# One inference step of a two-layer mLSTM and pooling decoder on one core: a rebuilt beginning, and accumulators read one by one

## The chip, the core and the metric

The kernel runs on one core of a Trainium2 chip. Its engines are TensorE (PE, with the weight loads listed apart as PEld), VectorE (DVE), ScalarE (ACT), GpSimd (POOL) and SyncE (SP, which only issues DMAs here); each runs its own list of instructions in order, and semaphores tie the lists together. The metric is the device time of one execution in microseconds (us): the median of three runs of the kernel before is 2596.98 us (2596.16 to 2598.49).

## The reference, cut to what matters

One step of a decoder with two layers, on a prompt (16 meta tokens and 256 prompt tokens) and on a sample group (8 sequences of 8 tokens): 336 columns in all, each of width D = 2048. Layer 0 mixes tokens by an mLSTM (4 heads, keys of 256, values of 512, with a matrix state C per sequence), layer 1 by pooling; behind each stands a gated feed-forward network (FFN) of width 5504 with a short convolution.

```python
def trunk(x, ...):
    for layer in range(DEPTH):
        u = rms_norm(x, norm_mix[layer])
        if layer % 2 == 0:
            y, (C, n, m) = mlstm_mixer(u, w_mlstm_in, b_mlstm_gate, g_mlstm_out, w_mlstm_out, (C, n, m), lead)
        else:
            y, pbuf = pool_mixer(u, st_pool, pos0, w_pool, pool_scale)
        x = x + y
        u = rms_norm(x, norm_ffn[layer])
        y, cbuf = conv_ffn(u, st_conv, w_up, conv_w, conv_b, w_down)
        x = x + y
    out = rms_norm(x, norm_final)

def mlstm_mixer(u, w_in, ...):
    q, k, v, o, gates = split(u @ w_in)          # gates: 4 input and 4 forget gates per column
    ig, lf = gates[:H] + b, log_sigmoid(gates[H:] + b)
    # running sums of lf, running maxima m_t (the stabilisers), scores exp(d - m_t), state C, n
```

For the beginning this matters: u is x over its root mean square per column times a gain per feature, and the gates, with all the row tables of running sums and maxima made from them, need u @ w_in for eight columns of w_in. All of it is float32.

## The kernel before, in words

**Products.** x is held with features on partitions (16 blocks of 128 features, 336 columns). The product of a weight block with x is made in three passes of TensorE over split numbers: a weight w is split into a high half wh and the rest wl, x into xh and xl, and wh·xh, wh·xl and wl·xh are summed (lines 433 to 435). The gain of the norm is multiplied into xh and xl, while the factor per column (one over the root mean square, `rbc`) is applied when an accumulator is read.

**Chunks.** Weights come in chunks of 256 rows by 512 columns (0.5 MB), by SyncE's `chunk` (line 287), into four slots. ScalarE writes the high half of a chunk (`hi`, line 814), VectorE the low half (`lo`, line 1081), and each counts a semaphore: `raw_landed`, `hi_done`, `lo_done`, and `chunk_used` once TensorE is done with it. `gemm` works through the chunks of a product; each chunk is 24 passes, six for each of four accumulators, SA[0..3] or SB[0..3] (the eight banks); products alternate between SA and SB.

```python
                for i in range((nkt + 1) // 2):
                    if amid and i in amid:
                        amid[i]()
                    s = (k0 + i) % SLOTS
                    pe.wait_ge(lo_done, c + (k0 + i + 1))
                    if fresh:
                        fresh(2 * i)
                    for t in range(nt):
```

`amid[i]` is other work of TensorE put ahead of chunk i, `guard` and `free` are waits of an accumulator's first pass, and `fresh` waits for the split x. A head of the mLSTM is a product of eight chunks for q and k (SA, chunks 0 to 7), one of eight for v (SB, chunks 8 to 15), one for the output gate (SA, 16 to 23), and four of two chunks each for the output projection. VectorE reads accumulators in order and counts `evac`; before the change it begins on the four of a product when `chunk_used` says that the last chunk is done, as in `add_to_x` (line 1100), which adds the output projection or an FFN's down projection to x.

**The beginning.** SyncE issues five DMAs for x with tokens on rows, in whole rows (lines 299 to 303), twelve for the parameters of norms, convolutions and the normaliser state n (`in_par`, lines 304 to 314), those of the gates (`in_gate`, 315 to 321), then chunks. TensorE transposes x (line 472) as the three row blocks arrive, then the parameters (477 to 484); it makes the gates, eight columns of w_in spread over 36, in full float32 (490), and sums squares over the features by 16 products with a matrix of ones (494). Only then comes the first `gemm`. ScalarE writes four chunk halves and then, by turns, the high half of a block of x and its square (857 to 865); VectorE copies the transposed x out of the banks (1103 to 1107), scales the gate weights (1120), and writes chunk halves and the low half of x. The row tables (1127 to 1143, tables of 4 rows by 336) wait once for ScalarE's exp and ln (868, 871). Head 0's TensorE list then turns the row tables into columns (`stabilisers`, ahead of chunk 5).

**Later places that the change touches.** Line 513, in `new_states`: the products of the new state C of the previous head, which stand between the chunks of a head's q and k product. Line 628: the products of the prompt's state, between the output gate product and the output projection; they wait for accumulators SA[2] and SA[3]. Lines 1334 and 1337: VectorE's read of an FFN's second product (`fh`) and the low half made of it (`hl`), which the down projection takes. Line 799: the final transposes; line 782: the last sums of squares of the second norm, with a sum made on GpSimd (line 1486).

## Time and profile before

| | |
|---|---|
| median of three runs | 2596.98 us |
| the profiled execution | 2595.99 us |
| its span (first to last instruction in the trace) | 2593.6 us |
| TensorE busy | 98% of the span |
| VectorE, ScalarE, GpSimd busy | 53%, 38%, 7% |
| first pass over a weight chunk starts at | 46.07 us |

All times in a trace count from the start of the span. The profiled execution lasted 2.4 us longer than its span: what lies ahead of its first and behind its last instruction. A row of a timeline gives the start and the duration of an instruction, or of a run of like ones, its engine and line, its tiles (written<-read) and, in brackets, how long the engine stood idle ahead of it and what ended that. Passes of TensorE are pipelined: one is listed with 0.3 to 0.6 us, but the next starts before it ends; so a cost per pass is taken from a stretch over a count and not from the duration of one.

### The profile page before, as it was taken

To read this page: it belongs to the slowest core of one execution; us is meant where nothing else is said; L and a number is where in the kernel's file an instruction comes from. 1 tells how busy PE (TensorE), PEld (TensorE's weight loads), DVE (VectorE), ACT (ScalarE), POOL (GpSimd) and SP (SyncE) were. 2 spreads that over 40 slices of the span, in tenths; PEclk is the share of its full clock that TensorE was granted. 3 is DMA by queue.
4 is the path that set the end of the run, shared out by engine and by line. 5 is a ranking of instruction groups with operands and counts; after the bars stand their busy time and mean duration, and the time that the engine had idled before them with its cause. 6 is when DMAs were issued, how large, how long until landed. Compare 5 with 4: busy or idle time off the path is not lost. (4 is left out here: it accounts for less than half of the span.)

```text
span 2593.6 us, 43931 instructions
## 1 busy us (share of the span) xinstructions
PE 2554.5 (98%) x16751; PEld 2481.2 (96%) x16751; DVE 1364.6 (53%) x2095; ACT 976.1 (38%) x1284; POOL 172.8 (7%) x338
## 2 busy tenths in 40 slices
PE   7999999999999999999999999999999999999998
PEld 5989898998999999999999999999999999999998
DVE  5445464547654454544544546755554554545545
ACT  4332323235432333433333335543333333433435
POOL 1000000002060000000000002300000000000002
PEclk9999999999999999999999999999999999999999
DMA  4637364563544444444444444344444444444443
GB/s 129 203 113 253 102 225 137 158 216 109 202 142 144 142 144 140 137 151 147 142 145 142 144 127 149 117 147 149 155 148 154 149 149 150 143 161 151 148 136 109
DMA packets 226617, 389.63 MB, mean 150 GB/s; under 512 B 25564, under 2 KB 55636, under 8 KB 225876
## 3 DMA queue, kind: packets, MB, share of 16 engines
q1 hardware_dynamic: 214683, 367.26, 44.5%
q10 hardware_dynamic: 11736, 19.67, 2.1%
q8 instruction: 132, 2.16, 0.3%
q14 instruction: 66, 0.54, 0.1%
HBM read 363.86 MB, written 23.43 MB: 149 GB/s over the span
## 5 line engine op out<-in xcount | busy, mean ns | idle before, releaser
L1081 DVE TENSOR_TENSOR w_lo<-w_raw,w_hi 128x1024 fp32r<-128x1024 f32 x664 | 814.8, 1233 | 971.4 <-ACT w_hi L814 968.9
L814 ACT ACTIVATE w_hi<-w_raw 128x1024 fp32r<-128x1024 f32 x664 | 700.0, 1059 | 1356.2 <-PE bank L435 1325.7
L433 PE MATMUL bank<-xh,w_hi 128*128 128x336 f32 (+2 forms) x3584 | 1131.9, 316 | 0.7 <-DVE w_lo L1081 0.5
L434 PE MATMUL bank<-xl,w_hi 128*128 128x336 f32 (+2 forms) x3584 | 1125.3, 314 | 0.0
L435 PE MATMUL bank<-xh,w_lo 128*128 128x336 f32 (+2 forms) x3584 | 1123.5, 313 | 0.0
L433 PEld LDWEIGHTS bank<-xh,w_hi 128*128 128x128 f32 x3584 | 673.1, 188 | 17.5 <-issue 15.4
L434 PEld LDWEIGHTS bank<-xl,w_hi 128*128 128x128 f32 x3584 | 674.2, 188 | 1.2 <-issue 1.0
L435 PEld LDWEIGHTS bank<-xh,w_lo 128*128 128x128 f32 x3584 | 674.9, 188 | 0.0
L433 PE MATMUL bank<-hh,w_hi 128*128 128x336 f32 (+1 forms) x1632 | 513.0, 314 | 4.5 <-issue 4.5
L435 PE MATMUL bank<-hh,w_lo 128*128 128x336 f32 (+1 forms) x1632 | 511.4, 313 | 0.0
L434 PE MATMUL bank<-hl,w_hi 128*128 128x336 f32 (+1 forms) x1632 | 511.2, 313 | 0.0
L433 PEld LDWEIGHTS bank<-hh,w_hi 128*128 128x128 f32 x1632 | 306.9, 188 | 6.0 <-issue 6.0
L434 PEld LDWEIGHTS bank<-hl,w_hi 128*128 128x128 f32 x1632 | 307.4, 188 | 1.0 <-issue 1.0
L435 PEld LDWEIGHTS bank<-hh,w_lo 128*128 128x128 f32 x1632 | 307.9, 189 | 0.0
L1526 POOL COPY area<-area 128x18 f32<-128x18 f32 x86 | 37.1, 434 | 1703.2 <-DVE area L1313 1703.2
L1100 DVE TENSOR_TENSOR x<-bank,x 128x336 f32<-128x336 f32 (+1 forms) x256 | 110.4, 494 | 69.3 <-PE bank L435 69.3
L974 ACT ACTIVATE area<-area 128x352 f32<-128x352 f32 (+1 forms) x86 | 42.4, 493 | 58.3 <-DVE area L1321 58.3
L980 ACT ACTIVATE hh<-area 128x336 fp32r<-128x336 f32 (+1 forms) x86 | 36.5, 478 | 67.1 <-DVE area L1334 67.1
L1481 POOL TENSOR_TENSOR area<-area 128x336 f32<-128x336 f32 x58 | 57.7, 995 | 33.9 <-ACT area L842 26.9
L1288 DVE SCALAR_TENSOR_TENSOR area<-area,bank 128x512 f32<-128x512 f32 x64 | 43.6, 744 | 20.0 <-PE bank L513 19.9
L969 ACT ACTIVATE area<-area,cp 128x352 f32<-128x352 f32 (+1 forms) x86 | 50.9, 663 | 5.8 <-DVE area L1313 5.8
L1334 DVE TENSOR_TENSOR area<-bank,area 128x336 f32<-128x336 f32 (+1 forms) x86 | 37.0, 492 | 27.7 <-PE bank L435 27.7
(268 smaller groups left out, 1021.0 us busy)
## 6 DMA issues: line engine op xcount, KB each, us to landing
w_raw<-in_w_up SPq DMA_DIRECT2D x640, 256.0 KB, 2.8
w_raw<-in_w_down SPq DMA_DIRECT2D x336, 256.0 KB, 3.4
w_raw<-in_w_mlstm_in SPq DMA_DIRECT2D x192, 256.0 KB, 3.4
area<-in_state_mlstm_C SPq DMA_DIRECT2D x32, 512.0 KB, 7.4
w_raw<-in_w_mlstm_out SPq DMA_DIRECT2D x64, 256.0 KB, 3.2
out_C_sample<-area ACTq DMA_DIRECT2D x32, 512.0 KB, 5.8
w_raw<-in_w_up SPq DMA_DIRECT2D x64, 192.0 KB, 2.5
w_raw<-in_w_pool SPq DMA_DIRECT2D x16, 256.0 KB, 3.0
```

What stands on the lines that cost most here:

```text
L433: pe.matmul(out, wh, xhk, start=first, stop=False)
L434: pe.matmul(out, wh, xlk, start=False, stop=False)
L435: return pe.matmul(out, wl, xhk, start=False, stop=last)
L814: nc.scalar.activation(w_hi[:, s], w_raw[:, s], ACT.Copy).then_inc(hi_done, 1)
L969: nc.scalar.activation(Tt[:, t, a0:GW - 2], E[:, t, a0 + 2:GW], ACT.Identity, bias=cp[:, 3, 4 * q + t:4 * q + t + 1], scale=cp[:, 2, 4 * q ...
L974: nc.scalar.activation(Tt[:, t, a0:GW - 2], Tt[:, t, a0:GW - 2], ACT.Silu).then_inc(silu_ready, 1)
L1081: V.tensor_tensor(w_lo[:, s], w_raw[:, s], w_hi[:, s].bitcast(F32), ALU.subtract).then_inc(lo_done, 1)
L1100: V.tensor_tensor(x[:, 4 * n + t, c0:], banks[t][:, c0:T], x[:, 4 * n + t, c0:], ALU.add).then_inc(evac, 1)
L1288: V.scalar_tensor_tensor(Cr[b][:, k], Cr[b][:, k], WI[:, NS * b + NS - 1:NS * b + NS], SB[s][:, :], ALU.mult, ALU.add).then_inc(c_updated, 1)
L1334: V.tensor_tensor(fh[:, t, a0:], SB[t][:, a0:T], Sp[:, t, a0:], ALU.mult).then_inc(evac, 1)
L1481: m_ = G.tensor_tensor(sums[k], sums[k], squares[k][:, kt % 4], ALU.add)
L1526: m_ = G.tensor_copy(last[:, q, 0:nt * ROWS].rearrange("p (b s f) -> p b s f", s=2, f=nt)[:, :, :, t], E[:, t, NP - NS:].rearrange("p (b s ...
```

## The change

**The beginning.** SyncE brings x in three pieces of columns (features 0 to 511, 512 to 1023, 1024 to 2047), with two q and k chunks of head 0 between them; the gates' weights, the convolution tables and n stand behind chunks 5 and 6, and the norms' parameters are issued by ScalarE. TensorE turns the identity 22 times, the norms' parameters and the first quarter of x, and goes into head 0's q and k product; the other three quarters of x stand ahead of its chunks 1, 2 and 3, the gates ahead of chunk 5, the row scales ahead of chunk 6 and the remaining parameters ahead of chunk 7. The gates are now summed in four strips of 32 columns (each strip over four of the 16 blocks), copied out by ScalarE and added by one more product with a table `pick`. The sum of squares of a column is made by ScalarE on x with tokens on rows (`row_squares`, the sum beside the square), its root and inverse on three columns, and TensorE spreads the inverse over all partitions by a product with a diagonal (`row_scales`). The column tables (`columns`) move behind the end of the q and k product, ahead of the v product's chunk 1, and the scores from chunk 2 of the v product to chunk 4.

**Reads one by one.** TensorE counts `acc_done` after the last pass of each accumulator of a product but the last one, and VectorE waits for that count ahead of each read (`summed`) and no longer for the end of the whole product. This is done for all products of the heads, the FFNs and the pooling layer. The first product of line 628 now waits for the third read of four, and the order of reads at the output gate becomes 0, 1, 2, 3.

```diff
+            def x_piece(p):
+                cols = PIECES[p]
+                for rows, s, src in ((slice(0, META), 0, I["meta_tokens"]), (slice(META, P), 0, I["x_prompt"][0, 0:P - META]),
+                                     (slice(0, P), 1, I["x_prompt"][0, P - META:2 * P - META]),
+                                     (slice(0, META), 2, I["x_prompt"][0, 2 * P - META:SEQ]),
+                                     (slice(META, TL), 2, I["x_sample"].rearrange("b s d -> (b s) d"))):
+                    sp.dma_start(xtok[rows, s, cols], src[:, cols]).then_inc(in_x[p], 16)
...
+            x_piece(0)
+            qk_chunk(0, 0, 0)
+            qk_chunk(0, 0, 1)
+            x_piece(1)
+            qk_chunk(0, 0, 2)
+            qk_chunk(0, 0, 3)
+            x_piece(2)
+            qk_chunk(0, 0, 4)
+            qk_chunk(0, 0, 5)
...
+            qk_chunk(0, 0, 6)
+            for i in range(2):
...
+                        if i == (nkt + 1) // 2 - 1 and t < nt - 1:
+                            mm_.then_inc(acc_done, 1)
...
+            def to_features(q):
+                pe.wait_ge(in_x[min(q, 2)], 16 * 5)
+                for s, (t0, m) in enumerate(TOK):
+                    n = 3 * q + s
+                    if n == 3:
+                        pe.wait_ge(st_ev, 1)
+                    elif n > 3:
+                        turned(n - 4)
                     for t in range(4):
                         kt = 4 * q + t
-                        m_ = pe.transpose(bank[(4 * s + q) % 8][:, t * P:t * P + n], xtok[0:n, s, kt * P:(kt + 1) * P],
-                                          ident[0:n, 0:n])
+                        m_ = pe.transpose(SB[n % 4][:, t * P:t * P + m], xtok[0:m, s, kt * P:(kt + 1) * P], ident[0:m, 0:m])
                     m_.then_inc(st_tr, 1)
...
+            def gates():
+                turned(9)
+                turned(10)
+                turned(11)
+                pe.wait_ge(wgg_ready, 1)
+                for k in range(KT // 4):
+                    for s in range(4):
+                        kt = 4 * k + s
+                        m_ = pe.matmul(SB[3][32 * s:32 * s + 32, 0:T], wgg[:, kt, :], x[:, kt, :], start=(k == 0),
+                                       stop=(k == KT // 4 - 1), skip_group_check=True)
+                m_.then_inc(gates_mm, 1)
+            def row_scales():
+                pe.wait_ge(rdiag_ready, 1)
+                for s, (t0, n) in enumerate(TOK):
+                    m_ = pe.matmul(SB[0][:, t0:t0 + n], ones[0:n, :], rdiag[0:n, s, 0:n], start=True, stop=True)
+                m_.then_inc(rbc_mm, 1)
...
+            def parameters():
...
+            for _ in range(WARM):
+                pe.transpose(SA[0][:, 0:P], ident[:, :], ident[:, :])
+            pe.wait_ge(in_par, 16 * 5)
+            pe.transpose(SB[3][:, 0:7 * KT], ptok, ident[0:7 * KT, 0:7 * KT]).then_inc(st_tr, 1)
+            to_features(0)
...
+                def columns():
+                    pe.wait_ge(rows_ready, 1)
+                    pe.wait_ge(evac, e + 4)
...
+                if first:
+                    gemm(SA, c, 0, KT, 4, xh, xl, 0, fresh=lambda kt: pe.wait_ge(xl_done, kt + 2),
+                         amid={1: lambda: to_features(1), 2: lambda: to_features(2), 3: lambda: to_features(3), 5: gates,
+                               6: row_scales, 7: parameters})
+                    guard = {0: (r_ready, 1), 1: (rows_ready, 1), 2: (st_ev, 10), 3: (st_ev, 11)}
...
-                gemm(SB, c, 8, KT, 4, xh, xl, 0, free=None if first else after(e - 4), guard=guard, amid={2: scores})
+                gemm(SB, c, 8, KT, 4, xh, xl, 0, free=None if first else after(e - 4), guard=guard,
+                     amid={1: columns, 4: scores} if first else {2: scores})
...
-                    pe.wait_ge(evac, e + (8 + (1, 4)[k]))
+                    pe.wait_ge(evac, e + (8 + (3, 4)[k]))
...
+                for s, (t0, n) in enumerate(TOK):
+                    if p + s:
+                        act.wait_ge(row_sq, 3 * p + s)
+                    nc.scalar.activation(spent[0:n, 0:cols.stop - cols.start], xtok[0:n, s, cols], ACT.Square,
+                                         accum_out=parts[0:n, s, p:p + 1]).then_inc(row_sq, 1)
...
+            hi(0, 0)
+            gather(0)
+            x_high(0)
+            hi(0, 1)
+            hi(0, 2)
+            gather(1)
+            x_high(1)
+            act.wait_ge(consts, 2)
+            row_squares(0)
+            hi(0, 3)
+            gather(2)
+            x_high(2)
+            row_squares(1)
+            hi(0, 4)
+            gather(3)
+            x_high(3)
+            hi(0, 5)
+            row_squares(2)
+            hi(0, 6)
+            act.wait_ge(row_sum, 1)
+            nc.scalar.activation(rtok[:, 1], rtok[:, 0], ACT.Sqrt, bias=eps[:, :], scale=1.0 / D).then_inc(rt_ready, 1)
+            hi(0, 7)
...
+            def summed(t, nt, a, c):
+                if t < nt - 1:
+                    dve.wait_ge(acc_done, a + (t + 1))
+                else:
+                    dve.wait_ge(chunk_used, c)
...
+            def add_to_x(banks, n, c0, a, c):
                 for t in range(4):
+                    summed(t, 4, a, c)
...
+            lo(0, 5)
+            dve.wait_ge(row_sq, 9)
+            step(V.tensor_tensor(rtok[:, 2], parts[:, :, 0], parts[:, :, 1], ALU.add))
+            V.tensor_tensor(rtok[:, 0], rtok[:, 2], parts[:, :, 2], ALU.add).then_inc(row_sum, 1)
             dve.wait_ge(in_gate, 16 * 5)
             dve.wait_ge(consts, 2)
...
+            V.tensor_tensor(wgg[:, :, 0:8], wgr, par[:, 0:KT].unsqueeze(2).to_broadcast([P, KT, 8]), ALU.mult).then_inc(wgg_ready, 1)
+            lo(0, 6)
...
+                los(c, 9, 11)
                 if first:
                     dve.wait_ge(cleared, 1)
...
-                dve.wait_ge(chunk_used, c + 8)
                 for t in range(4):
+                    summed(t, 4, a, c + 8)
...
+                if first:
+                    dve.wait_ge(gcol_mm, 1)
+                    V.tensor_copy(gcol[:, :].rearrange("p s a h -> p (s a h)"), SA[1][:, 0:24]).then_inc(gcol_a, 1)
+                    lo(c, 12)
+                    dve.wait_ge(gcol_em, 1)
+                    scales(h, SA[3])
...
-                    dve.wait_ge(chunk_used, c + (k0 + nd))
-                    add_to_x((SA, SB)[n % 2], n, a0)
+                    add_to_x((SA, SB)[n % 2], n, a0, a + (ab + 3 * n), c + (k0 + nd))
```

TensorE's list from its start to the first weight passes, before (each row an operation, its tiles, its shape and how often it stands there in a row):

```order
L428 UNCONDITIONAL_BRANCH
L472 MATMUL bank<-ident,area 128x128 x32
L472 MATMUL bank<-ident,area 128x80 x16
L477 MATMUL bank<-ident,area 128x112
L480 MATMUL bank<-ident,area 128x86 x4
L484 MATMUL bank<-ident,area 128x32 x2
L490 MATMUL bank<-x,area 36x336 x16
L494 MATMUL bank<-area,ones 128x336 x16
L433 MATMUL bank<-xh,w_hi 128x336
```

The same stretch after the change:

```order
L458 UNCONDITIONAL_BRANCH
L553 MATMUL bank<-ident 128x128 x22
L555 MATMUL bank<-ident,area 128x112
L514 MATMUL bank<-ident,area 128x128 x8
L514 MATMUL bank<-ident,area 128x80 x4
L463 MATMUL bank<-xh,w_hi 128x336
```

48 transposes of x, the gates and 16 products for the sums of squares stood ahead of the first weight pass (L433 before, L463 after); now 12 transposes of x do, and the rest has moved between the chunks or, with the sums of squares, off TensorE.

ScalarE's list from its start, before (L814 is a chunk's high half, L860 the high half of a block of x, L863 a block's square):

```order
L804 UNCONDITIONAL_BRANCH
L814 ACT_TABLE_LOAD
L814 ACTIVATE w_hi<-w_raw 128x1024 x4
L860 ACTIVATE xh<-x,par 128x336
L863 ACTIVATE area<-x 128x336
```

After the change, from the chunk halves 1 and 2 to chunk half 3 (L884 is a chunk's high half, L932 the copy of transposed sample columns, L941 the high halves, L950 the squares of x by rows):

```order
L884 ACTIVATE w_hi<-w_raw 128x1024 x2
L932 ACTIVATE x<-bank 128x4x80
L941 ACTIVATE xh<-x,par 128x336 x4
L950 ACTIVATE area,parts<-area 128x512 x2
L950 ACTIVATE area,parts<-area 80x512
L884 ACTIVATE w_hi<-w_raw 128x1024
```

Where four chunk halves stood at the head of the list, chunk halves, the copies and high halves of a quarter of x, and the squares of a piece now alternate; the squares of the last piece stand behind six chunk halves (the diff has the whole order).

VectorE's list between the row tables and the reads of head 0's q and k product, before (L1149 is the last step ahead of the stabilisers, L1081 a chunk's low half, L1153 the copy of the column tables, L1166 to L1170 the scalings made from them, L1178 the first read of a q accumulator):

```order
L1149 TENSOR_SCALAR mrows<-mrows,negeye 4x336
L1081 TENSOR_TENSOR w_lo<-w_raw,w_hi 128x1024 x5
L1153 COPY gcol<-bank 128x24
L1157 COPY hcol<-gcol 128x6
L1158 COPY mbh<-mb 128x8
L1159 COPY nh<-nT 128x16
L1160 COPY gh<-par 128x4
L1166 TENSOR_SCALAR area<-bank,hcol 128x272
L1167 TENSOR_SCALAR area<-bank,hcol 128x144
L1168 TENSOR_SCALAR area<-bank,hcol 128x16
L1169 TENSOR_SCALAR area<-bank,hcol 128x4x16
L1170 TENSOR_TENSOR area<-bank,mbh 128x64
```

After the change (L1295 and L1297 copy the convolution tables and n, L1303 is the step ahead of the stabilisers, L1202 a chunk's low half, L1315 and L1316 the first of the reads):

```order
L1295 COPY cpar<-bank 128x344
L1297 COPY nT<-bank 128x64
L1303 TENSOR_SCALAR mrows<-mrows,negeye 4x336
L1202 TENSOR_TENSOR w_lo<-w_raw,w_hi 128x1024 x2
L1315 SCALAR_TENSOR_TENSOR area<-bank,rbc 128x272
L1316 SCALAR_TENSOR_TENSOR area<-bank,rbc 128x4x16
```

Five chunk halves and the scalings stood between the row tables and the reads; now two chunk halves do, and the copy of the column tables with the scalings has moved behind the reads (the last but one piece of the diff).

## Rows read from the trace of the kernel before

**Rows 1.** Page of before: busy us, share of span and instructions of each engine.
```profile
PE 2554.5 (98%) x16751; PEld 2481.2 (96%) x16751; DVE 1364.6 (53%) x2095; ACT 976.1 (38%) x1284; POOL 172.8 (7%) x338
```

**Rows 2.** Busy time by stretches: start:end, length, each engine (instructions), clock, DMA share, GB/s.
```profile
23.84:46.00 22.16, 22.09 (x63) 9.37 (x64) 13.78 (x20) 18.14 (x37) 0.96 (x1) 0.91 0.53 167
46.00:77.20 31.20, 31.20 (x204) 30.39 (x203) 18.70 (x35) 14.46 (x17) 0.00 (x0) 1.00 0.38 114
77.20:109.30 32.10, 32.10 (x212) 31.94 (x212) 13.76 (x24) 9.36 (x10) 2.23 (x4) 1.00 0.77 253
1581.00:1584.40 3.40, 3.40 (x14) 3.40 (x13) 1.03 (x1) 0.00 (x0) 0.00 (x0) 0.50 0.24 77
```

**Rows 3.** Timeline of TensorE, beginning: sample rows of x turned; first weight product.
```profile
13.01 1.33 PE L472 MATMUL bank<-ident,area 80*128 80x80 f32 x16 [0.26 <-DMA area<-in_x_sample]
...
46.07 0.57 PE L433 MATMUL bank<-xh,w_hi 128*128 128x336 f32 x1
```

**Rows 4.** Groups of TensorE instructions, 0 to 110 us: busy, mean, idle before.
```profile
L490 PE MATMUL bank<-x,area 128*36 128x336 f32 x32 | 11.2, 519 | 2.9 <-DVE area L1120 2.9
...
L472 PE MATMUL bank<-ident,area 128*128 128x128 f32 x32 | 5.4, 350 | 7.3 <-POOL area L1468 7.3
...
L477 PE MATMUL bank<-ident,area 112*128 112x112 f32 x1 | 0.4, 448 | 5.2 <-DMA area<-in_state_mlstm_n 5.2
```

**Rows 5.** Waits of TensorE over the span: us in total, times, longest.
```profile
PE bank L513 <- DVE x L1100: 3.0, 4, 1.8
...
PE bank L628 <- DVE area L1258: 2.8, 4, 0.7
```

**Rows 6.** Timeline of TensorE, down projection of FFN 0: start, us, line, [idle].
```profile
1580.24 0.39 PE L433 MATMUL bank<-hh,w_hi 128*128 128x336 f32 x1 [2.31 <-issue]
...
1581.39 0.48 PE L433 MATMUL bank<-hh,w_hi 128*128 128x336 f32 x1
...
1581.67 0.48 PE L434 MATMUL bank<-hl,w_hi 128*128 128x336 f32 x1
```

**Rows 7.** Timeline of TensorE at the end of the kernel.
```profile
2577.70 1.42 PE L799 MATMUL bank<-ident,x 128*128 128x128 f32 x11 [0.36 <-DVE x L1100]
...
2580.78 0.98 PE L782 MATMUL bank<-ones,area 128*128 128x1 f32 x6 [1.66 <-POOLq L1486]
```

**Rows 8.** DMA, 0 to 40 us: GB/s in 40 slices of one microsecond.
```profile
GB/s 0 41 188 295 319 279 287 410 442 164 221 143 54 17 40 25 45 59 53 4 1 46 214 325 324 303 378 370 238 357 168 335 254 286 285 300 45 0 0 0
```

**Rows 9.** Groups of ScalarE instructions by shape, 0 to 130 us.
```profile
L814 ACT ACTIVATE w_hi<-w_raw 128x1024 fp32r<-128x1024 f32 x23 | 24.2, 1057 | 61.7 <-PE bank L435 37.4 <-DMA w_raw<-in_w_mlstm_in 24.3
...
L860 ACT ACTIVATE xh<-x,par 128x336 fp32r<-128x336 f32 x16 | 8.9, 559 | 0.0
...
L910 ACT ACTIVATE area<-bank 128x512 f32<-128x512 f32 x2 | 1.2, 597 | 2.6 <-PE bank L584 1.5 <-PE bank L586 1.1
```

**Rows 10.** Groups of VectorE instructions by shape, 0 to 110 us.
```profile
L1081 DVE TENSOR_TENSOR w_lo<-w_raw,w_hi 128x1024 fp32r<-128x1024 f32 x19 | 23.1, 1224 | 26.7 <-ACT w_hi L814 26.5
...
L1090 DVE SCALAR_TENSOR_TENSOR xl<-x,par,xh 128x336 fp32r<-128x336 f32 x16 | 9.0, 568 | 5.1 <-ACT xh L860 5.1
...
L1106 DVE COPY x<-bank 128x512 f32<-128x512 f32 x8 | 5.2, 686 | 8.9 <-PE bank L472 8.9
```

**Rows 11.** Groups of TensorE instructions by shape: products into strips of 32 columns.
```profile
L598 PE MATMUL bank<-area 128*32 128x512 f32 x128 | 14.6, 595 | 0.0
```

**Rows 12.** Timeline of VectorE: first, middle and last row of the row tables.
```profile
51.12 0.50 DVE L1130 SCALAR_TENSOR_TENSOR area<-area 4x336 f32<-4x336 f32 x1
...
54.06 0.50 DVE L1132 SCALAR_TENSOR_TENSOR area<-area 4x336 f32<-4x336 f32 x1 [2.44 <-ACT area L869]
...
58.30 0.18 DVE L1142 COPY area<-mtrow 4x64 f32<-4x64 f32 x1
```

**Rows 13.** Timeline of VectorE ahead of the down projection after FFN 0.
```profile
1577.97 1.34 DVE L1334 TENSOR_TENSOR area<-bank,area 128x336 f32<-128x336 f32 x3 [0.41 <-PE bank L435]
...
1579.22 1.33 DVE L1337 TENSOR_TENSOR hl<-area,hh 128x336 fp32r<-128x336 f32 x3
```

352 lines of the change are left out of this document (190 added, 162 removed).

## The prediction

> **What bounds the kernel now.** I read the busy shares first: TensorE is busy 98% of the span, no other engine over 53% [rows 1]. So only time in which TensorE does something else than weight products, or waits, can be won. The windows by stage come next. In 46 to 77.2 us (head 0's q and k product) and 77.2 to 109.3 us (its v product) TensorE has no idle time at all [rows 2]; each window holds eight chunks of 24 products. The first product of a weight starts only at 46.07 us, though [rows 3]: 46 of 2593.6 us pass in getting ready. Of these, 22.2 us (23.84 to 46) are TensorE working, but on the gates and on the column sums of squares [rows 2], 32 passes of 11.2 us for the gates alone [rows 4]; and 5.2 us are a wait for the last of the parameter DMAs [rows 4]. That is the stage that the first part of the change rebuilds. The second part touches the ends of the products, and there the list of waits says what can be had: TensorE waits 2.8 us at line 628 and 3.0 us at line 513 for VectorE's reads of accumulators, in four places each [rows 5], some 2.3 us ahead of the last down projection of an FFN [rows 6], and little at the end [rows 7].
>
> **The first part, as a new timetable up to the end of head 0's v product (before: 109.3 us).** I lay the new order of each engine over durations of these rows.
>
> *Until the first weight product.* The DMAs move, in KB by microsecond, 41, 188, 295, 319, ... [rows 8]: 0.52 MB by 4 us, 1.12 MB by 6, 1.41 MB by 7. Columns 0 to 511 of x are 0.69 MB, chunk 0 behind them 0.52 MB: moved by 4.6 and 6.3 us. Before, all 2.75 MB of x are moved at about 11.9 us and TensorE is released at 13.0 [rows 3, 8], so a landing is seen about 1.1 us later: 5.7 and 7.4 us. TensorE meanwhile turns the identity 22 times and the parameters once (32 passes took 5.4 us, 0.17 each [rows 4]: 3.9 us), then the first quarter of x: 12 transposes, 2.0 us, done at about 8.4. ScalarE splits chunk 0 (1.06, to 8.5), copies the sample columns (about 0.5, to 9.0) and writes two high halves of x (0.56 each [rows 9], to 10.1). VectorE copies two groups (0.69 each), writes the low half of chunk 0 (1.22) and two low halves of x (0.57 each [rows 10]) to about 11.0. First weight product: 11 us instead of 46.
>
> *What TensorE then has to do up to the end of the v product.* The two windows of before, 31.2 + 32.1 = 63.3 us [rows 2], hold all that is still there (the small transposes of the row tables and the stabilisers' broadcast move from the first to the second). New between the chunks are: three quarters of x to turn, 36 transposes, 36 x 0.14 = 5.0 us (between 0.17 and the 0.11 that transposes take later on); the gates in four strips; the row scales (4 small products, 1.2 us); the last parameters (6 transposes, 1.0 us). The gates are 16 products of two passes. Passes of 32 columns in strips took 14.6 us for 128 of 512 columns [rows 11], 0.114 each, by 336/512 that is 32 x 0.075 = 2.4 us; if the strips do not run side by side, it is the 11.2 us of before [rows 4]. I take 2.4. Sum: 63.3 + 9.6 = 72.9; without a wait the v product ends at 84.
>
> *Waits that come in.* (a) The gates now stand ahead of chunk 5 and need the gate weights times the norm's gain, which VectorE writes only after ScalarE's ninth row square. ScalarE's list up to there: 6 chunk halves (1.06), 4 copies (0.5), 16 high halves (0.56), 6 squares of 512 columns (0.60 and reading the sum [rows 9], 0.7) and 3 of 1024 (1.2), 25 us less some 2.5 for overlap. It starts at 7.4 and is stopped about 9 us more, because it waits in its own order for transposes of quarters that TensorE issues only between chunks, and twice for VectorE's copies, queued behind a chunk's low half: 39 us, the gate weights at 39.6. TensorE is there at 11 + 5 x 3.7 + 5.0 = 34.5. Wait 5.0 (0 if ScalarE isn't stopped, 10 if twice as long). (b) Accumulator 1 of the v product waits for the finished row tables. Before, that chain took from 51.1 to 58.5 us, 2.44 of it waiting for ScalarE's exp and ln [rows 12]; now a chunk half stands in that gap on each engine. From the row scales (46.9 us) I come to 56.6, TensorE is there at 56.1: wait 0.6. (c) The column tables are turned ahead of chunk 9 and need all four q and k accumulators read. VectorE does the row tables to 56.6, two copies and a scaling (1.0), two chunk halves (2.4) and only then the four reads (2.0): 62.0. TensorE is there at 59.4: wait 2.6. Behind it, nothing but chunk 9 and the products after it. Together with 0.4 for a late chunk: 8.6 us.
>
> *The clock.* In 23.84 to 46 us the granted clock averages 0.91, in the two product windows it is 1.00; after the idle 2.3 us ahead of 1580.24 [rows 6] it is 0.50 for 1581 to 1584.4 [rows 2], half speed, 1.2 GHz. There 14 products took 3.40 us and not the 0.153 each of 46 to 77.2: 1.3 us lost. The new beginning has gaps of 2.4 us (8.4 to 11), 5.0 and 2.6: two or three such stretches, 3 us (0 to 9).
>
> End of the v product: 11 + 72.9 + 8.6 + 3 = 95.5, against 109.3: **13.8 us won** (19 without the clock's part and wait (b, c); 6 with the clock low through five chunks more).
>
> *What is hidden.* The 32-byte gate weights and the tables now stand between chunks 5, 6 and 7 on SyncE's queue. Before, that group ran at 4 to 59 GB/s for 9 us (12 to 21 us [rows 8]). From 14 us that makes chunk 7 land at about 28; ScalarE reaches it at 41. Only with 13 us more would it cost.
>
> **The second part: reads one by one.** The first three accumulators of a product end 2.8, 1.8 and 0.9 us before the fourth, and a read takes 0.45 [rows 13]; so behind the last product one read is left where there were four (or three). Line 628: its first product needs the third read, its second set the fourth: the 2.8 us [rows 5] go. Line 513: of 3.0 us I take 2.0; in one place low halves of x stand on VectorE ahead of it. Last down projections: three reads (1.34 us) and then the low halves [rows 13] become one read: 1.1 us twice, 2.2, and the stretch at 0.50 after the first of them in one case of two, 0.7. End: the last square and with it the sum on GpSimd come 1.2 us earlier of the 0.36 and 1.66 waited [rows 7]. Sum 8.9 us. From below it is 0 (if what TensorE waits for next is just as late), from above 12. VectorE now sits in an open wait between reads; behind it stand chunk halves, which had been behind the same reads before, so none gets later.
>
> **Sum.** 13.8 + 8.9 = 22.7. The profiled execution took 2595.99 us (span 2593.6), the median of the runs is 1.0 above it: 2596.98 - 22.7, about 2574 us.
>
> A rule that speaks against the new beginning: the Trainium skill, "TensorE: Matmul & The Clock Gate", section "HAM oscillation — how this bites in real kernels", tells of a kernel whose bursts of products are parted by waits of a few microseconds and in which every burst starts at the low clock. The trace agrees in one place, 0.50 after 2.3 us of idleness [rows 2, 6]. The sum above carries it as 3 us; the second rival below is what it would do at its worst.
>
> **Rivals.**
> 1. Only the beginning pays; the reads one by one uncover the next wait. For it: TensorE's whole list of waits is short [rows 5]. Against it: after the reads come 12 products of line 628 that cover ScalarE's and VectorE's next work. Then 2597 - 13.8, about 2583.
> 2. Slower: in the new beginning TensorE never works long enough in one piece, and its clock stays at half through both products of head 0. At half clock products start 0.28 apart (1581.39, 1581.67 [rows 6]), so a chunk takes 24 x 0.127 = 3.05 us longer, 16 chunks 49, less the 8.6 of waits that it covers: the v product ends at 133, 24 later than before, and with 8.9 won the time is about 2612. It turns at ten or eleven cold chunks. Against it: the gaps lie between pieces of 18 us and more without a pause, and a slower TensorE leaves fewer gaps.
> 3. The gaps on ScalarE are longer (the squares, the strips not side by side, chunks late): some 8 us more before the gates or in them: about 2582.
> 4. Neither the clock nor waits (b) and (c) show: about 2567.
>
> **How the numbers follow.** The forecast has 0.70 with 2566 to 2581 as its own range; rival 1 has 0.09, rival 3 0.10, rival 4 0.07, rival 2 0.03, and 0.01 is left for no change. 2564 to 2586 holds the forecast, 1, 3 and 4 but for their tails, some 0.85. A difference under 0.2%, 5 us, can't be told from none: faster 0.95, same 0.02, slower 0.03.
>
> **What would show it.** The first weight product at 10 to 13 us; a wait of 3 to 7 us ahead of the gates; a wait of 1 to 4 ahead of the column tables; the end of the v product at 91 to 100; granted clock 0.5 in two or three stretches before 60 us and 1.0 from then on. Line 628 without a wait for VectorE; the idle time ahead of the last down projections at 1.2 and not 2.3. Wrong it is if the v product ends after 103, or if TensorE's waits after 110 us are no shorter than before.

## The result

The changed kernel takes 2578.31 us (median of four runs, 2577.53 to 2579.03) against 2596.57 us (2595.63 to 2598.49) of the kernel before on the same chip: 18.3 us or 0.7% less, a ratio of 0.9932 (95% interval 0.992 to 0.9944). Forecast were 2574 us and a range of 2564 to 2586; the gain was put at 22.7 us. The profiled execution took 2579.03 us, its span went from 2593.6 to 2577.0 us.

The page of the changed kernel, busy time and share of the span by engine; its counterpart is [rows 1]:

```profile
PE 2544.0 (99%) x16749; PEld 2480.5 (96%) x16749; DVE 1363.0 (53%) x2095; ACT 981.4 (38%) x1291; POOL 154.3 (6%) x332
```

TensorE is busy for 10.5 us less, of the 16.6 that the span lost; the rest was idle time. Where it came from is seen best by the same piece of work at the same point of both lists; the differences add up down the table:

| TensorE starts | before, us | after, us | ahead by |
|---|---|---|---|
| the first weight pass | 46.07 | 11.86 | 34.2 |
| head 0's `values` (the transposes of v), in its output gate product | 112.79 | 102.85 | 9.9 |
| head 0's prompt state | 154.19 | 143.40 | 10.8 |
| the last head's prompt state | 598.54 | 585.01 | 13.5 |
| the work behind FFN 0's down projection | 1602.12 | 1586.16 | 16.0 |
| the convolution tails in FFN 1's last pass | 2541.19 | 2524.91 | 16.3 |
| the transposes at the end | 2575.76 | 2560.70 | 15.1 |
| the end of the span | 2593.6 | 2577.0 | 16.6 |

The beginning gave 9.9 us, the places of the prompt state 0.9 us each, FFN 0's tail about 2; FFN 1's tail cost 1.2, and the end gave 1.5. Of FFN 0's tail about 1.3 us (14 passes in 3.40 us, at 0.153 each without the low clock [rows 2]) are half clock that stands there in the kernel before and not here; FFN 1's tail is the reverse. The last section shows that this differs between kernels with the same code at that place, so these two rows hold some chance. Rows of TensorE's timeline after the change (start, duration, instruction, in brackets the idle time ahead and what ended it), beginning:

```profile
11.86 0.39 PE L463 MATMUL bank<-xh,w_hi 128*128 128x336 f32 x1 [3.33 <-DVE xl L1211]
33.03 0.42 PE L463 MATMUL bank<-xh,w_hi 128*128 128x336 f32 x1 [0.99 <-DVE w_lo L1202]
41.32 4.71 PE L526 MATMUL bank<-x,area 128*32 128x336 f32 x32 [4.37 <-DVE area L1262]
...
61.31 0.42 PE L463 MATMUL bank<-xh,w_hi 128*128 128x336 f32 x1 [0.55 <-DVE area L1292]
66.68 0.19 PE L589 MATMUL bank<-ident,area 4*128 4x4 f32 x1 [2.33 <-DVE area L1320]
```

The first weight pass, where [rows 3] had 46.07, starts at 11.86; then come a late chunk, the wait for the gate weights (L1262 is their scaling), the row tables (L1292) and the reads of the q and k accumulators (L1320). The granted clock of the new beginning, in windows (start:end, length, busy time and count of TensorE, weight loads, VectorE, ScalarE, GpSimd, then clock, DMA share, GB/s), which answers to [rows 2]:

```profile
12.40:15.80 3.40, 3.40 (x14) 3.40 (x14) 2.18 (x3) 1.49 (x2) 0.00 (x0) 0.50 1.10 326
39.70:46.50 6.80, 5.18 (x34) 2.12 (x35) 3.88 (x9) 4.72 (x8) 0.00 (x0) 0.50 0.57 156
67.00:73.80 6.80, 6.80 (x25) 5.89 (x24) 4.63 (x16) 1.97 (x4) 0.00 (x0) 0.50 0.74 241
80.00:95.00 15.00, 15.00 (x102) 14.84 (x101) 5.87 (x7) 4.89 (x6) 3.79 (x4) 1.00 0.84 275
```

Three stretches at 1.2 GHz, each in or behind one of the gaps of 3.3, 4.4 and 2.3 us, 17 us in all. Two short ones, 3.4 us each, follow later, from 627 and from 2538 us, and the last 4.6 us of the span are at half clock too. The waits of TensorE (total, times, longest), to be laid beside [rows 5]:

```profile
PE bank L526 <- DVE area L1262: 4.4, 1, 4.4
PE bank L463 <- issue: 3.7, 2, 1.9
...
PE bank L574 <- DVE x L1229: 3.0, 4, 1.8
PE bank L589 <- DVE area L1320: 2.3, 1, 2.3
```

The wait of line 628 (L698 now) is gone; that of line 513 (L574 now) stands as before, 3.0 us.

### The profile page after: what moved, and what is told of

It reads as the page before. It is cut to its first block and busy times, and to the rows that moved or that the text cites. A ratio compares the mean times of both kernels' runs of the same rounds, so it can differ in the third digit from the quotient of the medians.

```text
span 2577.0 us, 44182 instructions
## 1 busy us (share of the span) xinstructions
PE 2544.0 (99%) x16749; PEld 2480.5 (96%) x16749; DVE 1363.0 (53%) x2095; ACT 981.4 (38%) x1291; POOL 154.3 (6%) x332
## 5 line engine op out<-in xcount | busy, mean ns | idle before, releaser
L1202 DVE TENSOR_TENSOR w_lo<-w_raw,w_hi 128x1024 fp32r<-128x1024 f32 x664 | 812.3, 1228 | 1064.7 <-ACT w_hi L884 1064.1
L884 ACT ACTIVATE w_hi<-w_raw 128x1024 fp32r<-128x1024 f32 x664 | 699.8, 1058 | 1360.8 <-PE bank L465 1350.2
L463 PE MATMUL bank<-xh,w_hi 128*128 128x336 f32 (+2 forms) x3584 | 1135.9, 317 | 5.4 <-DVE xl L1211 3.3
L463 PEld LDWEIGHTS bank<-xh,w_hi 128*128 128x128 f32 x3584 | 675.6, 189 | 24.7 <-issue 17.7
L463 PE MATMUL bank<-hh,w_hi 128*128 128x336 f32 (+1 forms) x1632 | 513.2, 314 | 3.7 <-issue 3.7
L463 PEld LDWEIGHTS bank<-hh,w_hi 128*128 128x128 f32 x1632 | 307.0, 188 | 5.2 <-issue 5.1
L1688 POOL COPY area<-area 128x18 f32<-128x18 f32 x86 | 22.7, 266 | 1717.1 <-DVE area L1469 1717.1
L1477 DVE SCALAR_TENSOR_TENSOR area<-area,cp 128x352 f32<-128x352 f32 (+1 forms) x86 | 49.6, 577 | 3.1
```

The lines of the kernel that those rows point to most:

```text
L463: pe.matmul(out, wh, xhk, start=first, stop=False)
L884: nc.scalar.activation(w_hi[:, s], w_raw[:, s], ACT.Copy).then_inc(hi_done, 1)
L1202: V.tensor_tensor(w_lo[:, s], w_raw[:, s], w_hi[:, s].bitcast(F32), ALU.subtract).then_inc(lo_done, 1)
L1477: V.scalar_tensor_tensor(Tt[:, t, a0:GW - 2], E[:, t, a0:GW - 2], cp[:, 0, f:f + 1], Tt[:, t, a0:GW - 2], ALU.mult, ALU.add).then_inc(taps ...
```

## The experiments

Each of these eight kernels is the changed kernel with the edit shown; lines that only follow from the ones shown are left out (in run one ScalarE's order and waits, in run seven which partitions are copied and added). The first four ran on one chip, the last four on another. The times of the kernel before that ran beside them are 2596.01 us (first four) and 2595.69 us (last four), so differences between the groups of runs are good to about 1 us. Executions of one kernel lie up to 5 us apart.

**One: the reads undone.** Theory: the change's two parts add up, and about half of what the reads give comes from the prompt state.

```diff
             def summed(t, nt, a, c):
-                if t < nt - 1:
-                    dve.wait_ge(acc_done, a + (t + 1))
-                else:
-                    dve.wait_ge(chunk_used, c)
+                dve.wait_ge(chunk_used, c)
...
-                    pe.wait_ge(evac, e + (8 + (3, 4)[k]))
+                    pe.wait_ge(evac, e + (8 + (1, 4)[k]))
...
-                for f in range(4):
+                for f in (2, 0, 1, 3):
                     summed(f, 4, a + 6, c + 24)
```

> The changed kernel with only its second part undone: VectorE again waits for the whole product ahead of the first read, and the read order at the output gate and the wait of the prompt's state products are those of before. Theory A (sizes read from the two traces: about 9.9 us come from the beginning, 3.6 from the four places of the prompt's state products, the rest of 16.6 from the tails and the end): about 2584.5 us, 6 to 7 above the changed kernel's 2578.3, the state products waiting 0.7 us each again. Theory B (the sizes of the forecast, 8.9 us for the reads): 2587. Theory C (the reads one by one bring nothing, all comes from the beginning): 2578.

Measured: 2585.72 us (2583.92 to 2588.17), ratio to before 0.9958 (0.9945 to 0.9972). So the beginning alone is worth 10.3 us (against the kernel before beside it) and the reads 7.4 (against the changed kernel) or 8.0 (what 10.3 leaves of 18.3). The list of waits has the prompt state's again:

```profile
PE bank L698 <- DVE area L1398: 2.8, 4, 0.7
```

The row has the number of [rows 5], in four places as there. The time lies between theory A (2584.5) and theory B (2587) and does not tell them apart; theory C and the forecast's first rival (only the beginning pays) are out.

**Two: the gate weights early.** One multiplication of VectorE is moved ahead of its wait for ScalarE's ninth row square, and also ahead of the low halves of x's last quarter and of chunk 5.

```diff
             gather(3)
+            dve.wait_ge(in_gate, 16 * 5)
+            dve.wait_ge(consts, 2)
+            dve.wait_ge(st_ev, 1)
+            V.tensor_tensor(wgg[:, :, 0:8], wgr, par[:, 0:KT].unsqueeze(2).to_broadcast([P, KT, 8]), ALU.mult).then_inc(wgg_ready, 1)
             x_low(0, 0, 0, 12, 16)
...
             V.tensor_tensor(rtok[:, 0], rtok[:, 2], parts[:, :, 2], ALU.add).then_inc(row_sum, 1)
-            dve.wait_ge(in_gate, 16 * 5)
-            dve.wait_ge(consts, 2)
-            dve.wait_ge(st_ev, 1)
-            V.tensor_tensor(wgg[:, :, 0:8], wgr, par[:, 0:KT].unsqueeze(2).to_broadcast([P, KT, 8]), ALU.mult).then_inc(wgg_ready, 1)
             lo(0, 6)
```

> The changed kernel with one instruction moved: VectorE scales the gate weights right after the copies of the last quarter of x, ahead of the low halves of that quarter and of chunk 5, no longer behind the nine row squares. Theory A (the wait ahead of the gates is VectorE's order alone, and the low clock in the gates follows from that wait): TensorE goes into the gates at about 37 us and not at 41.3, the 32 passes take about 2.3 us and not 4.7, some 1 us of wait appears ahead of the row scales; together 5 to 6 us, about 2573. Theory B (the strips take 0.56 us a round at any clock): 4.4 less 1, about 2575. Theory C (the row sums, not the gate weights, set the pace, and the wait only moves to the row scales): within 1 us of 2578.

Measured: 2569.13 us (2568.56 to 2573.47), 9.2 less than the changed kernel, ratio to before 0.9902 (0.9887 to 0.9917). TensorE's timeline, gates, row scales and column tables, and two windows:

```profile
37.94 2.47 PE L526 MATMUL bank<-x,area 128*32 128x336 f32 x32
45.09 0.90 PE L534 MATMUL bank<-area,ones 128*128 128x128 f32 x6 [0.77 <-DVE area L1267]
61.85 0.19 PE L589 MATMUL bank<-ident,area 4*128 4x4 f32 x1 [2.33 <-DVE area L1320]
```

```profile
59.60:61.80 2.20, 0.00 (x0) 0.00 (x0) 2.20 (x10) 0.00 (x0) 0.00 (x0) 1.00 0.85 221
61.85:69.00 7.15, 7.15 (x48) 6.69 (x49) 4.98 (x16) 2.92 (x5) 0.00 (x0) 1.00 0.72 236
```

The gates start without a wait and take 2.47 us, half of 4.71: that is the clock. The row scales wait 0.77 us, as expected. More came than theory A's 5 to 6 us, for the second window: TensorE stands still for 2.33 us ahead of the column tables as it did in the changed kernel, but here the clock stays at 1.00 behind it, some 3 us that were not counted on and that the edit was not meant to bring. Head 0's `values` start at 94.93 us, 7.9 earlier, and the lead is still 8.0 at the convolution tails of FFN 1's last pass (2516.94 us); the rest lies behind them, where the changed kernel has a stretch at half clock from 2538 us and this one none, though both wait 1.88 us there.

**Three: the gaps filled.** No wait is shortened; transposes that nobody reads keep TensorE at work.

```diff
             to_features(0)
+            for _ in range(28):
+                pe.transpose(SA[0][:, 0:P], ident[:, :], ident[:, :])
...
                 turned(11)
+                for _ in range(38):
+                    pe.transpose(SB[3][:, 0:P], ident[:, :], ident[:, :])
                 pe.wait_ge(wgg_ready, 1)
...
+                    pe.wait_ge(evac, e + 1)
+                    for _ in range(12):
+                        pe.transpose(SA[0][:, 0:P], ident[:, :], ident[:, :])
                     pe.wait_ge(evac, e + 4)
```

> The changed kernel with TensorE kept busy in its three gaps by transposes of the identity that nobody reads: 28 behind the first quarter of x, 38 ahead of the wait for the gate weights, 12 ahead of the column tables. No wait is shorter. Theory A (the three stretches at a granted clock of 0.50, from 12.4, 39.7 and 67.0 us, come from TensorE standing idle, and cost 1.5, 2.3 and 3 us): the clock stays at 1.00, the gates take 2.3 us, and the time falls by 5 to 7 us, to about 2572. Theory B (the clock falls for something else, for example at a set time after the start): the stretches at 0.50 stay and the time is within 1 us of 2578, or longer by what the transposes overrun.

Measured: 2573.95 us (2570.72 to 2575.97), 4.4 less than the changed kernel, ratio 0.9916 (0.9903 to 0.993). From the timeline and the windows of TensorE:

```profile
11.95 0.39 PE L463 MATMUL bank<-xh,w_hi 128*128 128x336 f32 x1 [0.19 <-DVE xl L1218]
22.74 1.37 PE L514 MATMUL bank<-ident,area 128*128 128x128 f32 x12 [1.92 <-DMA area<-in_x_sample]
37.80 4.31 PE L523 MATMUL bank<-ident 128*128 128x128 f32 x38
42.04 2.47 PE L528 MATMUL bank<-x,area 128*32 128x336 f32 x32
```

```profile
11.90:15.90 4.00, 3.95 (x26) 3.97 (x27) 2.19 (x3) 2.10 (x3) 0.00 (x0) 1.00 1.12 307
24.20:27.60 3.40, 3.40 (x14) 3.40 (x13) 2.75 (x6) 2.75 (x6) 0.00 (x0) 0.50 0.26 33
66.00:72.00 6.00, 6.00 (x40) 6.00 (x41) 3.83 (x15) 2.92 (x5) 0.00 (x0) 1.00 0.93 294
```

The gates start 0.7 us later than in the changed kernel and take 2.47 us: their 4.71 was the clock and nothing else. All three stretches at 0.50 are gone, and a new one stands behind a new gap: chunk 0, at full speed, brings TensorE to the third quarter of x before its last DMA has landed (1.92 us), and there the clock falls. Why 4.4 and not 5 to 7 us came is seen on VectorE, where the gate weights are scaled (the changed kernel's row first, then this run's):

```profile
40.88 0.29 DVE L1262 TENSOR_TENSOR area<-area,par 128x128 f32<-128x128 f32 x1
...
39.44 0.29 DVE L1269 TENSOR_TENSOR area<-area,par 128x128 f32<-128x128 f32 x1
```

They are ready 1.4 us earlier: after a chunk 0 at full speed the second quarter of x is turned at 15.73 us and not at 17.16, and ScalarE and VectorE keep that lead. TensorE, though, is at its 38 transposes until 42.04 us, 2.3 us after the weights are there (39.73). So the low clock in chunk 0 does cost 1.4 us, and the transposes that overrun give 2.3 away; without them some 6.7 us would have come, an estimate from these rows. The Trainium skill, "TensorE: Matmul & The Clock Gate", section "Part 4: PE-mode transpose", says that the full clock does not engage for transposes. This run does not agree: with 38 of them in 4.31 us the granted clock is 1.00 up to and through the gates, in the window below (whether they run in the mode that the page means, the trace does not tell).

```profile
37.80:44.45 6.65, 6.65 (x73) 5.03 (x70) 3.88 (x9) 4.75 (x8) 0.00 (x0) 1.00 0.61 173
```

**Four: chunk halves behind the reads.** What came of the reads in the output projection and in the FFNs' tails?

```diff
                 for n in range(4):
-                    los(c, 28 + 2 * n, 30 + 2 * n)
+                    lo(c, 28 + 2 * n)
                     add_to_x((SA, SB)[n % 2], n, 0, a + (9 + 3 * n), c + (26 + 2 * n))
+                    lo(c, 29 + 2 * n)
...
-                    los(c, k0 + 12, k0 + 19)
+                    tail = nt < 4
+                    los(c, k0 + 12, k0 + (18 if tail else 19))
...
+                    if tail:
+                        for f, t in ((product, 0), (product, 1), (low, 0), (low, 1), (product, 2), (low, 2)):
+                            f(t)
+                        lo(c, k0 + 18)
```

Here `product` is the read of an accumulator and `low` the low half made from it, both as they were.

> The changed kernel with VectorE's list changed at two places: in the output projection the low half of the later of two chunks stands behind the four reads and not ahead of them, and in the last pass of each FFN the low half of one chunk stands behind the reads, with the first two low halves of the activations ahead of the third read. Theory A (there the reads one by one could not begin early, because a chunk half stands ahead of them that waits for the end of the product itself): the 3.0 us of waits ahead of the new state's products, in four places, fall to about 0.5, the two idle times of 1.8 and 1.9 us ahead of the last down projections to about 0.8, and with the stretches at half clock that follow them the time falls by 4 to 6 us, to about 2573. Theory B (the next wait is just as late, a chunk's low half now): within 1 us of 2578.

Why it was expected is seen in the changed kernel's own trace: VectorE's timeline around the end of head 0's output projection (TensorE leaves its last product at 178.3 us), and ScalarE's:

```profile
179.50 1.23 DVE L1202 TENSOR_TENSOR w_lo<-w_raw,w_hi 128x1024 fp32r<-128x1024 f32 x1 [2.50 <-ACT w_hi L884]
180.64 1.74 DVE L1229 TENSOR_TENSOR x<-bank,x 128x336 f32<-128x336 f32 x4
```

```profile
178.41 1.06 ACT L884 ACTIVATE w_hi<-w_raw 128x1024 fp32r<-128x1024 f32 x1 [2.66 <-PE bank L465]
```

The low half needs ScalarE's high half, which needs the slot of the product's last chunk. It cannot run before the product ends, and the four reads stand behind it. Measured: 2572.44 us (2572.01 to 2575.14), 5.9 less than the changed kernel, ratio 0.9915 (0.9901 to 0.9928). VectorE at the same place, and the waits of TensorE at line 574 and ahead of the last down projections:

```profile
175.74 1.93 DVE L1229 TENSOR_TENSOR x<-bank,x 128x336 f32<-128x336 f32 x4
178.32 1.23 DVE L1202 TENSOR_TENSOR w_lo<-w_raw,w_hi 128x1024 fp32r<-128x1024 f32 x1 [0.65 <-ACT w_hi L884]
```

```profile
PE bank L574 <- DVE area L1445: 2.0, 1, 2.0
PE bank L463 <- issue: 1.6, 2, 0.8
```

The reads now run beside the product. The wait for them at line 574 is gone (one of 2.0 us for VectorE's state update is left), and 3.7 us ahead of the down projections became 1.6. Theory A; of the 5.9 us some 1.2 may be chance, since head 0's `values`, ahead of the first place that the edit touches, already start at 101.67 us and not at 102.85: the gates had half clock for 3.4 us only.

**Five: the three orders together**, the two above and the column tables ahead of chunk 10:

```diff
-                     amid={1: columns, 4: scores} if first else {2: scores})
+                     amid={2: columns, 4: scores} if first else {2: scores})
```

> The changed kernel with three orders changed together: the gate weights scaled early (the run before: 9.2 us), the chunk halves behind the reads in the output projection and in the last pass of each FFN (5.9 us), and the column tables turned ahead of chunk 10 and not of chunk 9, so that chunk 9 covers the reads that they wait for (2.3 us of idle time). Theory A (the three are independent waits of TensorE, so their gains add up): 2578.3 - 9.2 - 5.9 - 2.3, about 2561 us. Theory B (what is taken out of one place comes back as a wait for chunk halves or for the row tables in the next): above 2566.

Measured: 2561.23 us (2560.68 to 2562.26), 17.1 less than the changed kernel and faster than both kernels; ratio to before 0.9867 (0.9852 to 0.9882). The gains add up as expected, with the wait of 2.3 us alone counted for the third order; what that order gives by itself is in run eight. The windows from the gates to the first part of the output gate product:

```profile
37.60:40.10 2.50, 2.50 (x34) 1.04 (x34) 1.23 (x1) 2.44 (x6) 0.00 (x0) 1.00 0.07 20
60.00:66.00 6.00, 6.00 (x42) 5.32 (x41) 3.87 (x10) 1.16 (x2) 0.00 (x0) 1.00 0.48 140
66.00:92.00 26.00, 26.00 (x173) 25.84 (x172) 14.32 (x33) 8.76 (x11) 3.80 (x4) 1.00 0.96 328
```

TensorE is busy throughout 60 to 92 us, at full clock.

**Six: without the 22 transposes of the identity** (`WARM = 0`).

> The changed kernel without the 22 transposes of the identity at its start. Theory A (they only raise TensorE's clock, and the first quarter of x, then turned at half speed, still lies ahead of ScalarE's and VectorE's work on chunk 0): the first weight pass stays within 1 us of 11.9, the granted clock is 0.50 for longer in chunk 0, and the time is within 2 us of 2578. Theory B (without them TensorE stays at the low clock through several chunks, 3.05 us each): 2583 or more.

Measured: 2580.47 us (2577.86 to 2582.14), ratio 0.9939 (0.9925 to 0.9953); the changed kernel's 2578.31 is within its spread. The timeline of TensorE:

```profile
6.90 2.50 PE L514 MATMUL bank<-ident,area 128*128 128x128 f32 x12 [0.17 <-DMA area<-in_x_sample]
11.91 0.62 PE L463 MATMUL bank<-xh,w_hi 128*128 128x336 f32 x1 [2.51 <-DVE xl L1211]
```

The 12 transposes take 2.50 us instead of 1.37, all of it in the time that TensorE waits anyway; the first weight pass stays, and `values` start at 102.52, 0.3 earlier than in the changed kernel. The clock is not low for longer in chunk 0, as was expected: its first passes start 0.28 us apart until 15.13 us, in the changed kernel until 15.73. The 3 us by which this profiled execution (2582.14 us) ends later arise at two places that the edit does not touch, where its clock falls, from 633 and from 1568 us. The identity's transposes gain nothing here that could be measured: the clock that they raise is lost again in the gap ahead of chunk 0.

**Seven: the gates in one strip.**

```diff
-                for k in range(KT // 4):
-                    for s in range(4):
-                        kt = 4 * k + s
-                        m_ = pe.matmul(SB[3][32 * s:32 * s + 32, 0:T], wgg[:, kt, :], x[:, kt, :], start=(k == 0),
-                                       stop=(k == KT // 4 - 1), skip_group_check=True)
+                for kt in range(KT):
+                    m_ = pe.matmul(SB[3][0:32, 0:T], wgg[:, kt, :], x[:, kt, :], start=(kt == 0), stop=(kt == KT - 1))
```

> The changed kernel with its gates summed in one strip of 32 columns by 16 products one behind the other, as before, and not in four strips. Theory A (the four strips run side by side, so that a round of eight passes takes as long as two): the 32 passes take some 9 to 11 us as before the change and not 4.7, and the time rises by 4 to 6 us, to about 2583. Theory B (the strips bring nothing by themselves; VectorE and the row tables set the pace here): within 1 us of 2578.

Measured: 2586.24 us (2584.82 to 2586.78), 7.9 more than the changed kernel, ratio 0.9962 (0.9949 to 0.9976). TensorE's row, and the gates in two parts:

```profile
42.08 11.87 PE L524 MATMUL bank<-x,area 128*32 128x336 f32 x32 [4.35 <-DVE area L1259]
```

```profile
42.05:47.50 5.45, 5.42 (x10) 1.78 (x11) 3.31 (x6) 2.71 (x4) 0.00 (x0) 0.50 0.47 126
47.50:53.90 6.40, 6.40 (x24) 2.34 (x22) 0.00 (x0) 0.00 (x0) 0.00 (x0) 1.00 0.24 71
```

11.87 us against 4.71, 7.2 of the 7.9. Theory A in kind; the size was put too low, because the half clock falls on part of the longer piece too: its first 10 passes start 0.56 us apart, the other 22 0.28 (47.57 to 53.50 us; the 24 of the second row count two that began before it). At full clock 32 of them would take 9.0 us; in four strips they take 2.47.

**Eight: the column tables later**, the one line of the fifth run alone.

> The changed kernel with one change of order: the column tables are turned ahead of chunk 10 of head 0 and not of chunk 9. Theory A (TensorE waits there for VectorE's four reads, and the stretch at 0.50 from 67.0 us follows from that wait): no wait ahead of the column tables, no stretch at 0.50 after it, 2.3 + 2.7 us less, about 2573.5. Theory B (the low clock there comes back in another place, or the scores become late): 2576 or more.

Measured: 2572.62 us (2571.62 to 2574.78), 5.7 less than the changed kernel, ratio 0.991 (0.9894 to 0.9925). The column tables without a wait, and the clock behind them:

```profile
68.09 0.22 PE L589 MATMUL bank<-ident,area 4*128 4x4 f32 x1
```

```profile
68.00:76.00 8.00, 8.00 (x55) 7.45 (x54) 5.17 (x17) 2.92 (x5) 0.00 (x0) 1.00 0.77 243
```

The wait of 2.3 us and the stretch at half clock behind it are gone, and `values` start at 97.47 us, 5.4 earlier: the small wait cost more than twice its own length. The three gains taken alone, 9.2, 5.9 and 5.7, would be 20.8 and not the 17.1 of run five: run two was already without the half clock behind the column tables, so its 3 us are in both numbers.

No run takes the rebuilt beginning apart further: what x in pieces, the squares moved to ScalarE or the late parameters are worth by themselves is not shown.

## Why the prediction was right, and where it was not

The time lies in the range, and the mechanism was right: two parts of the gain, the first of them limited by waits at the places named. Its terms, in its own order:

- **First weight pass:** 11 forecast, 11.86 measured. The end of the v product: 95.5 forecast, 99.2 measured.
- **New work:** 36 transposes in three groups, put at 5.0 us, took 3.3 (1.1 from the end of a chunk to the next pass, three times); row scales 1.4 (1.2 forecast), parameters 0.6 (1.0). The gates, 2.4 at full clock: the two runs above show 2.47. In the changed kernel they take 4.71, for the clock.
- **Waits:** ahead of the gates 4.4 (5.0), for the row tables 0.55 (0.6), ahead of the column tables 2.3 (2.6); the late chunk 1.0 (0.4). That the gate weights stand behind the ninth row square was the reason given. It is half of it: VectorE waits 2.2 us for that square, and the rest is its own list, the low halves of x and of chunk 5 ahead of the scaling. Run two moves the scaling ahead of both and has no wait.
- **The clock, the term that was mis-sized:** 3 us were taken for two or three stretches as long as that of [rows 2], 3.4 us. Two of the three are 6.8 us long. In chunk 0 twelve passes start 0.28 apart and not 0.154 (1.5 us), the gates lose 2.2, and behind the column tables some 20 passes lose 2.5 and the small products 0.5 (1.37 us for these, 0.88 in run two): 6.7 us. The difference, 3.7, is nearly all that lacks between the 13.8 forecast for the beginning and the 9.9 of the trace. Run three shows that the part in chunk 0 counts: without it the gate weights are ready 1.4 us earlier. The errors of the other terms nearly cancel, and that is luck: with every term as measured (11.9, 63.3 for the two windows of before, 7.8 of new work, 8.3 of waits, 6.7 of clock) the sum is 98.0, and about 1 us of the 99.2 stands in no term.
- **Bursts and the low clock:** in the three gaps of the beginning the clock fell in or behind each, and it was back at 1.00 each time after 3.4 or 6.8 us, ahead of the next gap; it did not stay low, as the second rival had it. The third stretch lies at 67 us and two more at 627 and 2538 us, so the sign "before 60 us and 1.0 from then on" did not come true. The rule of the Trainium skill weighed in the prediction ("TensorE: Matmul & The Clock Gate", "HAM oscillation — how this bites in real kernels") agrees with these three places; the last section has gaps where it did not come true.
- **The reads:** 8.9 forecast, 7.4 to 8.0 by run one. Line 628 gave 0.9 four times, 3.6 (2.8 forecast). Line 513 gave nothing (2.0 forecast; 0.4 us in three heads and 1.8 in the last still stand), and the idle time ahead of the last down projections went from 2.3 to 1.8 and 1.9, not to 1.2. The end gave 1.5 (1.2). The failed step is "behind the last product one read is left where there were four": it looked at when accumulators are done and not at what stands ahead of the reads on VectorE. The prediction did name that queue, but only asked whether chunk halves would get later behind the reads. Run four moves them and gets 5.9 us.
- **FFN 1's tail:** here the changed kernel is 1.2 us worse. Its idle time is 0.35 shorter, but the clock falls behind it, which it did not do before. Run two waits as long there, and its clock stays up.
- **Arithmetic:** some side numbers of the forecast do not come out of its own terms: the gap from 8.4 to 11 us is 2.6 and not 2.4, 13.8 without clock and waits (b, c) is 20 and not 19, the fourth rival's time 2568 and not 2567, and the 6 for five more cold chunks cannot be worked out again. None of them enters the sum.

VectorE's timeline ahead of the last down projection of FFN 0, to be laid beside [rows 13], and TensorE's:

```profile
1562.45 1.23 DVE L1202 TENSOR_TENSOR w_lo<-w_raw,w_hi 128x1024 fp32r<-128x1024 f32 x1 [1.53 <-ACT w_hi L884]
1563.60 1.33 DVE L1490 TENSOR_TENSOR area<-bank,area 128x336 f32<-128x336 f32 x3
1564.85 1.33 DVE L1493 TENSOR_TENSOR hl<-area,hh 128x336 fp32r<-128x336 f32 x3
```

```profile
1565.86 0.39 PE L463 MATMUL bank<-hh,w_hi 128*128 128x336 f32 x1 [1.81 <-issue]
```

The product ends at 1564.05; the first of its three accumulators was done 1.8 us before, but VectorE was at a chunk half until 1563.68, and all three reads run in one piece as in [rows 13], only 0.4 us ahead of the product's end instead of behind it.

## What to carry to other kernels

A read that no longer waits for the whole product gains nothing while an instruction ahead of it in the same queue still does: look for the last wait of the queue, not of the instruction. A gap of two or three microseconds in a busy TensorE should be priced with the stretch at half clock that may follow it, here up to 6.8 us long and 3 us dear, and is best removed by an order that puts other work of TensorE over it. When a table is scaled or copied for TensorE, put that small instruction where its own inputs are there and not where its neighbours' are: here the place of one multiplication of 0.29 us cost about 5 us, its wait and the half clock in the gates; the other 4 of run two are stretches at half clock elsewhere that did not come.

## What the runs showed of the hardware that was not expected

- The same idle time at the same place does not always bring the low clock. Ahead of the column tables 2.33 us were followed by 6.8 us at 0.50 in the changed kernel, 2.33 us by none in run two. Ahead of the last down projections 2.31 us of idleness were followed by it in the kernel before [rows 6], and 2.23 us (FFN 1 of the same kernel) were not. Ahead of FFN 1's, 1.88 us were followed by it in the changed kernel and not in run two; ahead of FFN 0's, 1.81 us were followed by it in runs six and eight and not in the changed kernel or in runs two, three and seven. None of these five edits touches the FFNs. What decides was not settled by these runs. FFN 1 in the changed kernel and in run two, then FFN 0 in run six, first the timeline of TensorE and then windows behind the gaps:

```profile
2537.59 0.38 PE L463 MATMUL bank<-hh,w_hi 128*128 128x320 f32 x1 [1.88 <-issue]
...
2529.61 0.39 PE L463 MATMUL bank<-hh,w_hi 128*128 128x320 f32 x1 [1.88 <-issue]
...
1567.08 0.39 PE L463 MATMUL bank<-hh,w_hi 128*128 128x336 f32 x1 [1.81 <-issue]
```

```profile
2538.30:2541.70 3.40, 3.40 (x15) 3.40 (x14) 1.10 (x1) 0.00 (x0) 0.00 (x0) 0.50 0.31 96
...
2530.30:2533.70 3.40, 3.40 (x25) 3.40 (x25) 1.12 (x1) 0.25 (x1) 0.00 (x0) 1.00 0.32 96
...
1568.20:1571.60 3.40, 3.40 (x14) 3.40 (x13) 0.67 (x1) 0.00 (x0) 0.00 (x0) 0.50 0.25 80
```

- 32 passes in four strips of 32 columns take 2.47 us at full clock, in one strip 9.0 (worked out in run seven): 3.7 times less.
